# A 31-tap depthwise convolution in a two-block transformer kernel: three engines or VectorE alone

## The reference, cut to what matters

```
h = x + 0.5 * swiglu(rms(x), w1, w3, w2)          # 1024 -> 2816 -> 1024
p = rms(h) @ w_in                                 # u_conv 768, q 384, k 128, v 128, q_mem 256
y = a * sigmoid(gate)                             # the halves of u_conv: 256 positions x 384 channels
y_conv = silu(layer_norm(conv31(y) + b))          # depthwise, causal, 31 taps for each of 384 channels
y_swa = sliding_window_attention(rope(rms(q)), rope(rms(k)), v)       # 6 heads of 64
y_mem = memory_attention(rms(q_mem), rms(mem @ wk), mem @ wv)         # 4 heads of 64
h = h + concat(y_conv, y_swa, y_mem) @ w_out
h = h + 0.5 * swiglu(rms(h), w1, w3, w2)
x = rms(h)
```

## Time and profile before

| | |
|---|---|
| median of 3 runs | 1816.7 us (1816.16 to 1817.24) |
| the profiled execution: its own time, its span | 1823.1 us, 1821.8 us |
| TensorE matmul, busy | 1692.1 us, 93% of the span |
| VectorE, busy | 1283.1 us, 70% |
| ScalarE, busy | 910.1 us, 50% |
| GpSimd, busy | 235.9 us, 13% |
| first layer of the second block: gated input done to first head, heads | 952.2 to 998.5 us, 998.5 to 1051.7 us |
| second layer: the same | 1483.8 to 1530.1 us, 1530.1 to 1588.0 us |

### The profile page before, as it was taken

How to read it: one execution, slowest core, us unless ns; L and a number is a source line. 1 busy time by engine, 2 the same in 40 slices (tenths; PEclk the granted TensorE clock), 3 DMA queues, 4 the chain that set the end, 5 groups by cost and what they waited for, 6 DMA issues and landing times.

```text
span 1821.8 us, 23982 instructions
## 1 busy us (share of the span) xinstructions
PE 1692.1 (93%) x9824; PEld 1470.1 (81%) x9824; DVE 1283.1 (70%) x1551; ACT 910.1 (50%) x1165; POOL 235.9 (13%) x226
## 2 busy tenths in 40 slices
PE   6979899999999999999996689999999987789997
PEld 5769898888998888888886378888888876478886
DVE  6975567765657767677678757778777679567764
ACT  5544355444545554555445444556555454345543
POOL 0301010011101001000125210003100243110002
PEclk9999999999999999999998789999999997799999
DMA  6333335555434555455534015555555524035551
GB/s 265 139 139 116 139 139 185 187 189 208 159 115 162 187 212 193 178 186 188 204 128 162 23 47 208 185 214 186 185 187 193 184 96 162 0 116 185 185 186 68
DMA packets 42013, 291.05 MB, mean 160 GB/s; under 512 B 4784, under 2 KB 5040, under 8 KB 7600
## 3 DMA queue, kind: packets, MB, share of 16 engines
q1 hardware_dynamic: 40032, 282.61, 43.2%
q10 hardware_dynamic: 1872, 6.92, 1.0%
HBM read 288.46 MB, written 1.05 MB: 159 GB/s over the span
## 4 chain that ended last, share of the span: by engine, by line
PE 77%; DVE 16%; ACT 3%; issue 2%; POOL 1%; DMA 1%; SPq 0%; DVEq 0%; ACTq 0%; POOLq 0%
PE ps L277 36%; PE ps L276 18%; DVE w_lo L1280 5%; PE ps L274 4%; PE ps L265 3%; PE ps L267 2%; PE ps L266 2%; PE ps L414 2%; PE ps L275 2%; DVE arena L1801 2%; DVE xT L1288 2%; PE ps L310 1%; POOL stat L1907 1%; PE ps L311 1%; PE ps L312 1%
## 5 line engine op out<-in xcount | busy, mean ns | idle before, releaser
L1280 DVE TENSOR_TENSOR w_lo<-raw,w_hi 128x2048 fp32r<-128x2048 f32 (+1 forms) x272 | 616.4, 2269 | 217.2 <-ACT w_hi L797 213.4
L277 PE MATMUL ps<-xT,w_hi 128*128 128x512 f32 x1820 | 650.5, 397 | 0.0
L797 ACT ACTIVATE w_hi<-raw 128x2048 fp32r<-128x2048 f32 (+1 forms) x272 | 510.8, 1878 | 201.6 <-PE ps L277 117.9
L276 PE MATMUL ps<-xT,w_lo 128*128 128x256 f32 x1820 | 509.2, 280 | 0.3 <-DVE w_lo L1493 0.3
L277 PE MATMUL ps<-hT,w_hi 128*128 128x512 f32 x1168 | 412.5, 397 | 0.0
L277 PEld LDWEIGHTS ps<-xT,w_hi 128*128 128x128 f32 x1820 | 342.8, 188 | 70.8
L276 PEld LDWEIGHTS ps<-xT,w_lo 128*128 128x128 f32 x1820 | 344.4, 189 | 12.6 <-DVE w_lo L1493 0.6
L276 PE MATMUL ps<-hT,w_lo 128*128 128x256 f32 x1168 | 327.1, 280 | 1.7 <-DVE hT L1463 1.7
L277 PEld LDWEIGHTS ps<-hT,w_hi 128*128 128x128 f32 x1168 | 219.3, 188 | 51.0
L1940 POOL TENSOR_TENSOR ff<-ff 128x256 f32<-128x256 f32 x77 | 98.2, 1275 | 1050.0 <-ACT ff L827 668.1
L276 PEld LDWEIGHTS ps<-hT,w_lo 128*128 128x128 f32 x1168 | 220.3, 189 | 5.0 <-DVE hT L1463 2.9
(11 more groups left out here) (233 smaller groups left out, 2127.6 us busy)
## 6 DMA issues: line engine op xcount, KB each, us to landing
raw<-weights_dram SPq DMA_DIRECT2D x264, 1024.0 KB, 4.8
raw<-weights_dram SPq DMA_DIRECT2D x8, 384.0 KB, 3.2
tmp<-mem_dram ACTq DMA_DIRECT2D x2, 1024.0 KB, 6.6
x<-x_in_dram SPq DMA_DIRECT2D x2, 512.0 KB, 7.0
raw<-weights_dram SPq DMA_DIRECT2D x2, 512.0 KB, 9.0
arena<-mem_dram ACTq DMA_DIRECT2D x1, 1024.0 KB, 10.1
arena<-pool_mat_dram ACTq DMA_DIRECT2D x1, 1024.0 KB, 4.9
tmp<-masks_dram ACTq DMA_DIRECT2D x1, 768.0 KB, 16.4
```

The lines of the kernel that those rows point to most:

```text
L276: pe.matmul(ps[:, bank, 0:S], lo, src[:, k, 0, :], start=False, stop=False)
L277: return pe.matmul(ps[:, bank, :].rearrange("p (a n) -> p a n", a=2), hi, src[:, k, :, :], start=False, stop=last)
L797: act.activation(b.w_hi[:, s, 0:w], b.raw[:, s, 0:w], ACT.Copy).then_inc(*mark("hi", u))
L1280: dve.tensor_tensor(b.w_lo[:, s, 0:w], b.raw[:, s, 0:w], b.w_hi[:, s, 0:w].bitcast(F32), ALU.subtract).then_inc(*mark("lo", u))
```

## The change

The third channel block goes to VectorE. `run_taps` walks over 31 taps x 3 blocks (93 instructions in place of 62), its groups become 6 and 6, then six groups of 4, and 6 in each of the heads until they run out: nine heads with 6 and the tenth with 3. `terms` on ScalarE, `add_terms` on GpSimd, the four product buffers and TensorE's wait for GpSimd's last sum go away. 62 products on ScalarE and 62 additions on GpSimd (both layers together) are no longer there. Nothing else is moved.

```diff
         def chunk(k):
             if k == 0:
                 pe.wait_ge(*at("taps", l))
-                pe.wait_ge(*at("tap2", l, 30))
                 channel_sum(yc, "chsum")
...
-        def terms(n):
-
-            for _ in range(n):
-                j = next(others, None)
-                if j is None:
-                    return
-                if j == 0:
-                    act.wait_ge(*at("glu", l))
-                if j >= 4:
-                    act.wait_ge(*at("tap2", l, j - 4))
-                act.activation(b.term(j), yp[:, 2, j:j + S], ACT.Copy,
-                               scale=b.lp("conv_w")[:, 3 * j + 2:3 * j + 3]).then_inc(*mark("term", l, j))
-        terms(4)
...
-            terms(3)
             highs(u0 + L_MQ + i + 2)
...
-            terms(2)
             turned(tag, i, 2 + i % 2)
...
-        cw, taps = b.lp("conv_w"), iter([(j, ch) for j in range(31) for ch in range(2)])
+        cw, taps = b.lp("conv_w"), iter([(j, ch) for j in range(31) for ch in range(3)])
...
-                i.then_inc(*(mark("taps", l) if (j, ch) == (30, 1) else mark("tap", l, j, ch)))
-        run_taps(4)
+                i.then_inc(*(mark("taps", l) if (j, ch) == (30, 2) else mark("tap", l, j, ch)))
+        run_taps(6)
         lows(u0 + L_QK + 3)
-        run_taps(4)
+        run_taps(6)
...
             lows(u0 + L_MQ + i + 2)
-            run_taps(3)
+            run_taps(4)
...
         lows(u0 + L_MQ + 6)
-        run_taps(3)
+        run_taps(4)
...
         lows(u0 + L_MK + 3)
-        run_taps(3)
+        run_taps(4)
...
-            run_taps(4)
+            run_taps(6)
             if i >= 1:
                 close(i - 1)
...
-        def add_terms(j0, j1):
-            for j in range(j0, j1):
-                pool.wait_ge(*at("term", l, j))
-                if j:
-                    pool.wait_ge(*at("tap2", l, j - 1))
-                before = yc[:, 2, :] if j else b.lp("conv_b")[:, 2:3].broadcast_to([P, S])
-                i = pool.tensor_tensor(yc[:, 2, :], b.term(j), before, ALU.add)
-                i.then_inc(*mark("tap2", l, j))
-        add_terms(0, 4)
         head_roots(f"qk{l}", 16, 8)
-        add_terms(4, 16)
         head_roots(f"mq{l}", 32, 4)
-        add_terms(16, 19)
         head_roots(f"mk{l}", 64, 4)
-        add_terms(19, 31)
```

More of the change, by code:

```diff
@@ L150, in ptb @@
         return self.arena[:, {"at": 1, "xa": 13, "sw": 8}[tag[:2]], :]
-    def term(self, j):
-        at = 512 + 256 * (j % 2)
-        return self.arena[:, 5 + j // 2 % 2, at:at + S]
     def xr(self):
@@ L1184, in scalar_program @@
         act.activation(z6[:, 3:6, :], z6[:, 3:6, :], ACT.Sigmoid).then_inc(*mark("conv_sg", l))
-        others = iter(range(31))
-        def terms(n):
-            for _ in range(n):
-                j = next(others, None)
-                if j is None:
-                    return
-                if j == 0:
-                    act.wait_ge(*at("glu", l))
-                if j >= 4:
-                    act.wait_ge(*at("tap2", l, j - 4))
-                act.activation(b.term(j), yp[:, 2, j:j + S], ACT.Copy,
-                               scale=b.lp("conv_w")[:, 3 * j + 2:3 * j + 3]).then_inc(*mark("term", l, j))
-        terms(4)
         highs(u0 + L_QK + 3)
@@ L1998, in gpsimd_program @@
     for l in range(2):
-        z6, yp, yc, mu, var, lt = conv_views(b)
         fa, mx, fb = f"ffn1_{l}", f"mix_{l}", f"ffn2_{l}"
```

## The result

| | before | changed |
|---|---|---|
| median of the first five runs each | 1816.7 us (1816.16 to 1817.24) | 1824.8 us (1823.33 to 1825.29) |
| ratio | | 1.0043, 95% interval 1.0028 to 1.0058 |
| the profiled execution: time, span | 1823.1, 1821.8 us | 1825.1, 1823.8 us |
| VectorE, ScalarE, GpSimd busy | 1283.1, 910.1, 235.9 us | 1282.5, 884.8, 178.1 us |
| later, side by side on one chip: median | 1823.7 us (17 runs, 1817.2 to 1835.0) | 1824.7 us (12 runs, 1822.3 to 1828.0) |

I had forecast 1810.9 us. The first comparison says slower by 0.4%; the second, with more executions, says that there is no difference. The first five runs of the kernel before all lay at the lower edge.

A forecast was written before the change was run, and what follows sets the result against it. VectorE was taken to bound the way to the first head, slowed by GpSimd, with no engine near full in the heads. -3.6 + 0.7 = -2.9 us a layer, -5.8 for both, from 1816.7 to 1810.9; range 1804.5 to 1816.5.

The forecast's parts named there:

- The way to the first head: From the finished gated input to the first head: VectorE, freed from GpSimd's contention, arrives 3.6 us sooner a layer.
- The low part's load for unit 43: Before the first head: load and ScalarE's rounding of unit 43 stay hidden from VectorE, by under 1 us.
- VectorE's busy time: Whole kernel: hardly moves, about 29 us more for 62 taps less some 22 us of contention; within 15 us of 1283.
- The direct cost in the heads: Heads: two more taps a head hide in even heads, lie on the chain in odd ones; +0.7 us a layer.
- The tap's step: VectorE's taps outside GpSimd's runs: 0.40 us each, not the full 0.47 us, which would add 2 us in all.
- The clock in the heads: TensorE's granted clock in the heads: both layers stay as they were about half the time; first layer's worse 0.13.
- the ring: Heads: no engine is near full; the engines hand work round to one another.
- the signs of being wrong: Rotary steps at 1.1 us, unit 43 holding VectorE, odd-head waits for TensorE's matmuls, or grant under 0.65 in both layers.
- The reference level: Whole kernel: forecast starts from the runs' median of 1816.7 us, the profile taken as running 6.4 us above it.
- Contention is not what it looks like: Rival: rotary embedding and taps are slow by themselves, so nothing returns and each tap costs 0.4 us: 1832; chance 0.08.
- only the rotary embedding: Rival: only the rotary embedding is slow by itself, leaving -0.2 us a layer: 1816.3, no change; chance 0.07.
- TensorE's clock decides: Rival, heads: first layer becomes like the second, 1815.7, or second like the first, 1806.1; chance 0.13 each.

The follow-up runs named there:

- a_again: The changed kernel, unchanged, run many times beside the kernel before on the same chip: 1824.7 against 1823.7 us, ratio 1.000.
- a_even: The changed kernel with its taps in the heads dealt out as 8, 4, 8, 4 instead of 6, 6, 6, 6: 1818.0 us, ratio 0.996.
- a_early: Kernel before, but VectorE makes the third block's taps 0 to 11, ScalarE and GpSimd 12 to 30 in the heads: 1818.1 us, ratio 0.9961.
- b_look2: The kernel before, unchanged, run once more for a profile of the upper cluster of times: 1826.0 us.

## Why the prediction was wrong

- *The way to the first head*: right. Forecast -3.6 us a layer, measured -4.1 in both. The rotary steps went to 0.61 and 0.72, the taps to 0.40 a step, no group of six over 2.46 us. The low part's load for unit 43 did not hold VectorE either: ScalarE had rounded it at 978.33 and VectorE took it up at 979.27.
- *VectorE's busy time*: right, 1282.5 us. The sum of its terms gave some 7 us more (29 added, 22 returned), so what contention had added was nearer 30 us than 22.
- *The direct cost in the heads*: right, 0.7 forecast, 0.83 and 0.98 measured at equal clocks.
- *The tap's step*: right at 0.40 us. But the section of the Trainium skill that the prediction sets against the rows, VectorE: DVE Perf Modes, The DRAIN you can't avoid, also says that a next operation that is not held starts earlier. The rows agree with the section as a whole; it was read too narrowly.
- *The clock in the heads*: wrong, and this is the step that failed. The sum took the heads' clock as unchanged ("about half the time both stay") and put 0.13 on a worse first layer. The changed kernel had about 59 us of heads in all four layers seen; with the direct cost it should have had about 55. That is some 4 us a layer, 8 us in all, by the few layers profiled; by the times it is less, 5.6 us (6.5 gained with the clock kept up, 0.9 left against the mean of 1825.6). Either way it eats most of the 8.2 us gained ahead of the heads. The prediction took the clock's changes as a matter of chance, when the change moves the odds: it lengthens the pauses between TensorE's bursts (0.67 us ahead of head 4, where TensorE had gone on at once before). At half the clock TensorE's own bursts then set the ring's pace (3.21 and 4.46 us of waiting at the closes of heads 4 and 6). Of the signs of being wrong that the prediction names, one came, a grant under 0.65 in both layers: 0.60 and 0.65 here, the second at the bound itself, and 0.60 and 0.62 in a_again.
- *The reference level*: wrong, and by size the larger part of the miss. The forecast stands on 1816.7 us, and three runs within 1.1 us looked like a sharp level. Of the 76 later runs only nine lie at or under 1817.3, so five such runs in a row are hardly chance; what held them there stays open. The profile beside them was 6.4 us slower, and I called that a constant offset of the profiled execution. It was the sign that the program has several levels: the changed kernel's profile lies within its runs, with no offset. Against the 1825.6 us that the kernel before takes on average, the same sum gives 1819.8. The miss of 13.9 us is then 8.9 from the level and 5.6 from the clock in the heads, less 0.7 by which the instructions gave back more than the 5.8.
- *The rivals*: none of the three as it stood. "Contention is not what it looks like" and "only the rotary embedding" are refuted by the rows above. "TensorE's clock decides" named the mechanism, with too low a chance, without the case of both layers slow on the runs' own level (1810.9 + 4.8 + the same again is 1820.5, still 4 us short), and with its two directions taken as equal.

That the six-tap groups lower the grant is shown by a_even and a_early, which change them and gain 6.7 and 6.6 us; at equal grant 1.5 us of the first and nothing of the second are left for shorter work. That it is the longer pauses through which they do so rests on the one layer shown above. Which pause matters most was not tried.

## What to carry to other kernels

An engine that helps a busy one isn't free: here GpSimd's additions, off the path themselves, held up VectorE by 6.3 us a layer on the path, more than the work they took from it. Where engines hand short pieces round, ask what a change does to the pauses of TensorE and not only to the length of the chain; a few matmuls into an unused bank, placed in waits, took 9 us off the kernel before and, with the waits of the layer's end and the taps dealt out as 8 and 4, brought the changed one to 1800.5. And take a profiled execution that differs from the runs as a reading, not as an offset: run both kernels often and side by side before a difference of half a per cent is believed.

## What was not expected of the hardware

- The same program took 1816.1 to 1834.8 us on one chip, and of the 76 runs none lay between 1824.1 and 1827.6 (b_look2 did, at 1826.0). The Trainium skill, TensorE: Matmul & The Clock Gate, section What's actually happening, says that the monitor behind the clock runs freely; that agrees with the heads of one layer taking 51.92 us in one execution and 57.01 in another, at grants of 0.77 and 0.64.
- Extra work on TensorE made the kernels quicker: TensorE was busy for 41.92 us in the first layer's heads in place of 35.56, and they took 49.84 us in place of 53.18.
- VectorE and GpSimd alternated instruction by instruction at these sizes: a VectorE step that takes 0.60 us alone took 1.12, for as long as the additions ran.
